# Early w_ada products on TensorE, late ones on VectorE, projections begun on the first half of the positions, and bias tables made for all heads at once

## What is computed

```
def first_block(x, c, w_ada, b_ada, ...):
    mod = (c @ w_ada[l] + b_ada[l])[:, None, :]            # 1024 -> 6 * 1024
    sh_m, sc_m, gt_m, sh_f, sc_f, gt_f = jnp.split(mod, 6, axis=-1)
    h = rms_norm(x, g_pre_mix[l]) * (1.0 + sc_m) + sh_m
    z = h @ w_in[l]
    u, f, q, k, v = jnp.split(z, splits, axis=-1)
    y = concatenate([s5_mixer(u), fourier_mixer(f), window_attention(q, k, v)]) @ w_out[l]
    x = x + gt_m * rms_norm(y, g_post_mix[l])
    h = rms_norm(x, g_pre_ffn[l]) * (1.0 + sc_f) + sh_f
    ...                                                     # gated FFN with a convolution
def second_block(x, p, rel_bias, ...):
    ...                                                     # swiglu
    z = rms_norm_2(h, attn_pre_g[i]) @ w_in[i] + b_in[i]
    out_a = sink_swa_gqa(...)                               # 8 heads, band of 128
    out_b = dilated_mixture(...)                            # 8 heads, three dilated bands
    ...                                                     # w_out, swiglu, gated embedding
```

## Time and profile before

| | us |
|---|---|
| median of 3 runs | 4137.23 |
| lowest, highest | 4129.18, 4148.82 |
| the profiled execution's own time | 4134.44 |
| its span, first to last instruction | 4132.2 |
| mean granted TensorE clock | 0.921 of full |

### The profile page before, as it was taken

The page is one execution under the profiler, slowest core; times in us unless marked ns, Lnnn a source line. Parts: engine busy times, 40 slices in busy tenths (PEclk is TensorE's granted clock), DMA queues, the critical chain, the costliest instruction groups (busy, mean ns, idle before and its releaser), DMA issues.

```text
span 4132.2 us, 41174 instructions
## 1 busy us (share of the span) xinstructions
PE 3422.3 (83%) x15967; PEld 2832.5 (69%) x15967; DVE 1255.2 (30%) x1716; ACT 800.0 (19%) x1416; POOL 1625.7 (39%) x830
## 2 busy tenths in 40 slices
PE   3755233787999989989999998987777899999977
PEld 2654233566888878868888786876666788878865
DVE  6603556335233332130000123115544200011233
ACT  3011000433111112020000122016541200000222
POOL 4777866014233336523322563210015123335633
PEclk9977666799999999999999999989999999999988
DMA  5333000333111123311111332343433111123332
GB/s 181 125 107 99 7 7 7 87 125 102 41 51 51 51 97 112 102 53 49 51 51 43 136 122 85 133 145 93 109 103 121 41 51 41 51 74 115 115 140 86
DMA packets 249780, 347.06 MB, mean 84 GB/s; under 512 B 12390, under 2 KB 190865, under 8 KB 249650
## 3 DMA queue, kind: packets, MB, share of 16 engines
q1 hardware_dynamic: 212530, 237.95, 19.3%
q10 hardware_dynamic: 31712, 89.34, 5.8%
q0 software_dynamic: 5408, 18.02, 1.5%
HBM read 289.30 MB, written 55.95 MB: 84 GB/s over the span
## 4 chain that ended last, share of the span: by engine, by line
PE 72%; DVE 12%; ACT 5%; POOL 5%; issue 4%; DMA 1%; SPq 0%; ACTq 0%; DVEq 0%; POOLq 0%
PE PS L727 65%; PE PS L1703 3%; DVE pt L630 1%; POOL lacc L344 1%; DVE ot L1459 1%; DVE px L633 1%; DVE h_lo L716 1%; DVE pl_ab L1809 1%; POOL lw L342 1%; PE PS L1411 1%; DMA ada<-w_ada 1%; DVE oo L1460 1%; ACT act L608 1%; POOL act L342 1%; ACT ph_ab L1748 1%
## 5 line engine op out<-in xcount | busy, mean ns | idle before, releaser
L225 POOL CAST w_hi<-w_raw 128x2048 fp32r<-128x2048 f32 x173 | 335.5, 1939 | 1762.7 <-DMA w_raw<-ffn_w_gu 668.1
L227 POOL TENSOR_TENSOR w_lo<-w_raw,w_hi 128x2048 fp32r<-128x2048 f32 x181 | 859.5, 4749 | 36.6 <-ACT w_hi L1176 11.7
L727 PE MATMUL PS<-h_hi,w_hi 128*128 128x512 f32 x2464 | 763.4, 391 | 16.3 <-DVE h_lo L721 10.0
L727 PE MATMUL PS<-h_lo,w_hi 128*128 128x512 f32 x2464 | 762.1, 391 | 0.0
L727 PE MATMUL PS<-h_hi,w_lo 128*128 128x512 f32 x2464 | 761.0, 390 | 0.0
L727 PEld LDWEIGHTS PS<-h_hi,w_hi 128*128 128x128 f32 x2464 | 463.8, 189 | 113.4 <-issue 10.2
L727 PEld LDWEIGHTS PS<-h_lo,w_hi 128*128 128x128 f32 x2464 | 464.9, 189 | 96.8
L727 PEld LDWEIGHTS PS<-h_hi,w_lo 128*128 128x128 f32 x2464 | 464.1, 188 | 96.7
L727 PE MATMUL PS<-w_hi,a_hi 128*128 128x512 f32 x1056 | 328.6, 393 | 25.2 <-DVE a_lo L793 25.2
L936 DVE TENSOR_TENSOR aT<-act,PS 128x1024 f32 (+1 forms) x44 | 53.7, 1221 | 911.1 <-ACT act L916 911.1
L727 PE MATMUL PS<-w_lo,a_hi 128*128 128x512 f32 x1056 | 328.1, 392 | 0.0
(11 more groups left out here) (292 smaller groups left out, 4476.5 us busy)
## 6 DMA issues: line engine op xcount, KB each, us to landing
w_raw<-ffn_w_gu SPq DMA_DIRECT2D x88, 512.0 KB, 4.9
w_raw<-ffn_w_down SPq DMA_DIRECT2D x88, 512.0 KB, 4.2
w_raw<-w_up SPq DMA_DIRECT2D x44, 512.0 KB, 4.7
w_raw<-w_down SPq DMA_DIRECT2D x44, 512.0 KB, 4.2
xs<-px ACTq DMA_DIRECT2D x40, 512.0 KB, 3.0
px<-xs ACTq DMA_DIRECT2D x5, 4096.0 KB, 14.4
w_raw<-w_out SPq DMA_DIRECT2D x32, 512.0 KB, 4.5
w_raw<-w_in SPq DMA_DIRECT2D x28, 512.0 KB, 5.5
```

Source lines behind the costliest of these rows:

```text
L225: e.tensor_copy(w_hi[b][:, 0:n], w_raw[b][:, 0:n]).then_inc(S("w_hi"), 1)
L227: e.tensor_tensor(w_lo[b][:, 0:n], w_raw[b][:, 0:n], w_hi[b][:, 0:n].bitcast(F32), ALU.subtract)\
L727: mm = e.matmul(o, a[ai], b[bi], start=start and first, stop=stop and end)
```

## The change

1. The early 16 tiles are multiplied on TensorE: the columns of c go into `cz`, [128, 8, 2, 2], with the other half zero, and 32 matmuls with two output rows, 512 columns each, add both parts up in two PSUM banks. VectorE copies the two rows, eight small transposes make columns of them. `ada_dve` and two `mod_pe` go.
2. The late tiles are VectorE's (`late_dve`): one operation a tile in place of two. Their loads go from GpSimd's queue to SP's, between the loads of chunks (`late_sp`).
3. The norms ahead of both projections use eight PSUM banks, and the first two slots of the projections are done for positions 0 to 511 first; the last four sets of transposes come behind the first of these.
4. The tables: one product for all 16 heads (heads as rows), four pieces; two stores with the source row repeated 128 times.
5. Second attention: head 0's (and head 1's q) loads are issued on SP during the projections; ScalarE waits for the last stores after its first exp. `vbias` moves.

```
-        def late_pool(e, v):
...
+        def late_sp(e, first, end):
+            for i in range(first, end):
+                if i < 2:
+                    e.wait_ge(S("ht_lo"), 16)
+                else:
+                    e.wait_ge(S("lacc"), i - 1)
+                v, k = 2 + i // 8, i % 8
+                e.dma_start(lw[i % 2][:], t["w_ada"][0][k * P:(k + 1) * P, v * D:(v + 1) * D]).then_inc(S(f"lw_ld{i % 2}"), 16)
+
+        def late_dve(e, v):
+            if v > 2:
+                e.wait_ge(S("mod_mm"), v - 2)
             for k in range(KT):
                 i = (v - 2) * 8 + k
                 e.wait_ge(S(f"lw_ld{i % 2}"), 16 * (i // 2 + 1))
...
-                    e.tensor_scalar(lw[i % 2][:], lw[i % 2][:], vcol("c", k), None, ALU.mult).then_inc(S("lw_c"), 1)
-                    e.wait_ge(S("lw_c"), (v - 2) * 7 + k)
-                    e.tensor_tensor(lacc[:], lacc[:], lw[i % 2][:], ALU.add).then_inc(S("lacc"), 1)
+                    e.wait_ge(S("lacc"), i)
+                    e.scalar_tensor_tensor(lacc[:], lw[i % 2][:], vcol("c", k), lacc[:], ALU.mult, ALU.add)\
+                     .then_inc(S("lacc"), 1)
...
-            for i in range(2):
-                e.wait_ge(S("ada_c"), 8 * i + 8)
-                mod_pe(e, acc[i], PS[:, 7 - i, 0:8])
+            e.wait_ge(S("cz"), 3)
+            for i in range(16):
+                if i % 4 == 0:
+                    e.wait_ge(S(f"ada_ld{i // 4}"), 64)
+                for h in range(2):
+                    mm = e.matmul(PS[0:2, 6 + h, :], cz[:, i % 8, 1 - i // 8, :], ada[i][:, h * 512:(h + 1) * 512],
+                                  start=i == 0, stop=i == 15)
+            mm.then_inc(S("ada_mm"), 1)
+            for q in range(4):
+                norm_set(e, 0, q)
+            e.wait_ge(S("md2"), 1)
+            for k in range(KT):
+                mm = e.transpose(PS[:, 4, k * 2:k * 2 + 2], mod2[:, k * P:(k + 1) * P], ident[0:2, 0:2])
+            mm.then_inc(S("md_t"), 1)
+            for q in range(4, 12):
+                norm_set(e, 0, q)
...
         def z_pe(e, z):
-            e.wait_ge(S("ht_lo"), 16 * (1 if z == 0 else 4))
+            n = 0 if z == 0 else 3
+            first = [s for s in slots[0:2]]
+            for h in range(2):
+                for w, (c, _, c0, width, _, _, _) in enumerate(first):
...
+                    e.wait_ge(S("ht_lo"), n * 16 + 8 + 8 * h)
+                    for k in range(KT):
+                        mm = three(e, [PS[:, 2 * w + h, :]], ...)
+                    if h == 0 and w == 0:
+                        for q in range(12, 16):
+                            norm_set(e, n, q)
...
-        PIECES = [(h, c, min(c + 512, w)) for h in range(16) for w in [W_A if h < 8 else W_B] for c in range(0, w, 512)]
+        PIECES = [(0, 0, W_A)] + [(1, c, min(c + 512, W_B)) for c in range(0, W_B, 512)]
...
+            for k, w in enumerate((W_A, W_B)):
+                r = slice(8 * k, 8 * k + 8)
+                e.dma_start(tabd[r, :, 0:w], tst[k][r, :].unsqueeze(1).to_broadcast([8, P, w])).then_inc(S("tb_st"), 16)
...
         def out_act(e, p):
-                e.wait_ge(S("tb_st0"), 128)
-                e.wait_ge(S("tb_st1"), 128)
+                e.wait_ge(S("tb_st"), 32)
...
+        def att_first_sp(e, s, a):
+            e.wait_ge(S("tb_st"), 32)
+            ...
+            att_load_k(e, s, a, 0)
+            att_load_q(e, s, a, 0)
+            att_load_q(e, s, a, 1)
+            ...
+            att_load_v(e, s, a, 0)
...
             @block.sync
-                stream_load(e, NBUF, G_OUT1[0] + 2)
+                late_sp(e, 0, 2)
+                stream_load(e, NBUF, G_DFT)
+                late_sp(e, 2, 10)
+                stream_load(e, G_DFT, G_DFT + 1)
+                late_sp(e, 10, 18)
+                stream_load(e, G_DFT + 1, G_DFT + 2)
+                late_sp(e, 18, 26)
+                stream_load(e, G_DFT + 2, G_DFT + 4)
+                late_sp(e, 26, 32)
+                stream_load(e, G_DFT + 4, G_OUT1[0] + 2)
...
             @block.gpsimd
-                stream_split(e, 0, NBUF)
-                late_pool(e, 2)
...
-                stream_split(e, 5, G_GLU)
+                stream_split(e, 0, G_GLU)
...
             @block.vector
                 chain_dve(e)
+                late_dve(e, 2)
                 z_dve(e, 0)
```

More of the change, by code:

```diff
@@ L384, in gates_pe @@
             e.transpose(PS[0:16, 5, 0:P], gain1[:, 16:32], ident[:]).then_inc(S("gr_t"), 1)
[L386 to L396, removed]
         def mod_dve(e, n, v, src):
@@ L415, in prep_dve @@
             e.tensor_copy(vec[:, 0:NV], PS[:, 6, 0:NV]).then_inc(S("vc"), 1)
+            e.memset(cz[:], 0.0).then_inc(S("cz"), 1)
+            e.wait_ge(S("cz"), 1)
             e.wait_ge(S("vc"), 1)
-            ada_dve(e, 0)
+            for v in range(2):
+                e.tensor_copy(cz[:, :, v, v], vec[:, VC["c"]:VC["c"] + KT]).then_inc(S("cz"), 1)
             norm0_rows_dve(e)
@@ L421, in prep_dve @@
             e.tensor_scalar(cc[1][:], PS[:, 5, 0:SSM_W], -1.0, None, ALU.mult).then_inc(S("cc"), 1)
[L422 to L425, removed]
+            e.wait_ge(S("ada_mm"), 1)
+            e.tensor_copy(mod2[:], PSr[0:2, 3072:4096]).then_inc(S("md2"), 1)
+            e.wait_ge(S("md_t"), 1)
+            e.tensor_tensor(mod[:, 0:16].rearrange("p (v k) -> p k v", v=2), PS[:, 4, 0:16].rearrange("p (k v) -> p k v", v=2),
+                            vec[:, VC["b_ada"]:VC["b_ada"] + 16].rearrange("p (v k) -> p k v", v=2), ALU.add)\
+             .then_inc(S("mod_v"), 1)
+            e.wait_ge(S("mod_v"), 1)
             gain_pre_dve(e, 0, 1, "g_pre_mix")
@@ L672, in norm0_rows_dve, with norm_bank, norm_set @@
                 norm_scale_dve(e, 0, T)
-        def norm_pe(e, n):
-            for hf in range(2):
+        def norm_bank(n, q):
+            return q % 4 + (4 * (q // 8) if n in (0, 3) else 0)
+        def norm_set(e, n, q):
+            hf, k = q // KT, q % KT
+            if k == 0:
                 e.wait_ge(S("m_xn"), n * 4 + (hf + 1) * 2)
@@ L679, in norm_pe @@
                     e.wait_ge(S("n_tmp"), n * 8 - 2 if hf == 0 else n * 8)
[L680 to L688, removed]
+            if k >= 4 or (hf and n not in (0, 3)):
+                e.wait_ge(S("ht_f"), n * 16 + q - 3)
+                if n > 1:
+                    e.wait_ge(S("ht_lo"), n * 16 + q - 3)
+            for i in range(4):
+                mm = e.transpose(PS[:, norm_bank(n, q), i * P:(i + 1) * P], xn[:, hf * 4 + i, k * P:(k + 1) * P], ident[:])
+            mm.then_inc(S("ht_t"), 1)
+        def norm_pe(e, n):
+            for q in range(12 if n == 3 else 16):
+                norm_set(e, n, q)
         def norm_out_act(e, n):
@@ L1652, in att_sp @@
                 return
-            for par in range(2):
-                e.wait_ge(S(f"tb_st{par}"), 128)
-            for h in range(len(s.heads)):
+            for h in range(2, len(s.heads)):
                 att_load_k(e, s, a, h)
@@ L1769, in att_act @@
             exps(0)
+            for par in range(2):
+                e.wait_ge(S(f"z_st{par}"), z_stores(s.z, par))
             for m in range(s.n):
```

85 lines of the change are left out of this document (42 added, 43 removed).

## The result

The changed kernel takes 4046.87 us (median of 4 executions, 4039.11 to 4053.31) against 4143.02 of the kernel before in the same comparison: the ratio is 0.9773 with a 95% interval of 0.9754 to 0.9792. That is 2.3% faster: 96 us between the medians, 90 us between the two profiled executions (spans of 4132.2 and 4041.9). The forecast was 150 us less, 3985, and its range ended at 4045.

A forecast was written before the change was run, and what follows sets the result against it. GpSimd was taken to bound the first 400 us, mostly TensorE at full rate after. Terms -111 - 24 + 2 - 4 - 13 = -150 us from 4134.4 gave 3985; range 3945 to 4045.

The forecast's parts named there:

- Part 5: First attention's bias tables: 32 pieces become 4, -24 us; two added stores stay hidden, +2 us for crowding.
- Rival E: The two table stores run at 51 GB/s, end at 911 us, x comes 10 us late: 3993 us, chance 0.15.
- Parts 1 to 4: Start to the last Fourier product: -111 us, bounds -125 and -85, ending at 288 instead of 399.1 us.
- Part 1: Early w_ada products, moved to TensorE: the gain is there at 68 us, 7 us earlier.
- rival A: Early w_ada products: TensorE stays at 1.2 GHz, gain at 92 instead of 68 us: 4010 us, chance 0.10.
- Part 2: First projections start after 8 instead of 16 transposed sets, at 77 instead of 93.2 us; slot 7 at 157.
- Part 3: Late w_ada products on VectorE, 2.9 us a tile: projections stage ends near 212 instead of 296 us, 84 us less.
- rival B: Late w_ada tiles keep GpSimd's pace, 5.8 us; last Fourier chunk ends at 382: 4079 us, chance 0.07.
- Part 4: Fourier stage: DFT products begin at 229 us, chunk 9's load is late in SP's queue, last product at 288.
- Part 6: Second block: half start before the second projections, -4 us; head 0 loaded early for the second attention, -13 us.
- Rival C: The two table stores go through one engine of sixteen, x comes 207 us late: 4190 us, chance 0.03.
- D: Bias tables: the pieces filled TensorE's gaps, or the clock falls, and nothing is gained: 4009 us, chance 0.10.

The follow-up runs named there:

- tab_spread: Changed kernel with each head's table row made on 16 partitions, so the stores read all 128 partitions; 4003.5 us, ratio 0.9669 to the kernel before.
- tab_ports: tab_spread with the table stores reading eight partitions again, 16 apart instead of neighbours; 4007.6 us in one execution.
- tab_old: Changed kernel with the bias tables made as before (32 pieces, 16 stores from 128 partitions each); 4037.0 us, ratio 0.9768 to the kernel before.
- ada_dve: Changed kernel with the early w_ada products on VectorE again; Fourier stage ended at 305.5 us against 305.0, whole 4058.0 us in one execution.
- no_half: Changed kernel with both projections waiting for all 16 transposed sets again; Fourier stage ended at 300.6 us, whole 4032.7 us in one execution.
- best4: Changed kernel with tab_spread, sp_order and act_order together, without the half start in the first projections; 3996.9 us, ratio 0.966 to the kernel before.
- late_pool: Changed kernel with the late w_ada tiles back on GpSimd between its splits; Fourier stage ended at 388.8 us, whole 4129.3 us in one execution.
- act_order: Changed kernel with ScalarE's first two w_hi of the Fourier stage moved behind the eight copies into bd; 4040.4 us, ratio 0.9762 to the kernel before.
- sp_order: Changed kernel with DFT chunk 9's load ahead of the last six late loads in SP's queue, these in pairs between chunks; 4026.1 us, ratio 0.9718 to before.
- no_first: Changed kernel with head 0's loads of the second attention issued behind the stores again; 4054.1 us in one execution.

## Why the prediction was wrong

It forecast -150 us and -90 came. The direction and the main mechanism were right, and two terms of the sum were not.

**Part 5, 37 us, the larger miss.** The step that failed is "Hidden; I take +2 for crowding". The stores' time was bounded, from 15 to 246 us, and one figure was read off a store from 16 partitions, "at worst a third of the rate, some 50 us". It was 123 us. The two rows behind the figure, 60 KB and 192 KB, both landed in 1.9 us, so they tell no rate. Rival E had this rate, 51 GB/s, and even so its price, 3993, was 54 us too low (17 of them are parts 1 to 4). What was wrong is the way of pricing: it asked only when the stores end and whether x waits for them. They ended at 818 us and x did not wait. What they cost came while they ran: the loads of `tab_bi`, on SP's queue, took 24 us for 5, and ScalarE stood 10 us in the issue. tab_spread and tab_ports tie this to the stores: same place, same bytes, other source partitions, and the loads land in 4.8 and 12.4 us, the stretch takes 43 and 36 us less. That the loads are late because they share DMA engines with the stores is an inference: no record here names an engine. The other half of part 5 was sized low: 28 pieces gave 31 to 36 us, not 24.

**Parts 1 to 4, 17 us.** They are told step by step:
- Part 1 was right in its own terms (gain 69.2 for 68, 64.4 in tab_old; rival A, the low clock throughout, did not come) and worth little by the end of the Fourier stage: ada_dve. Part 2's first half brought nothing that shows there: no_half and best4. The step that failed is "So TensorE hardly stops": the sum counted 16 us of an earlier start down to the Fourier stage. It took VectorE's chain as 46 us from 85 on; it was 53 from 91.7 on, because the half start itself delays VectorE's last splits and GpSimd splits two chunks beside the small operations, not one. That made TensorE wait 4.9 us at slot 7 (3.4 to 4.9 in the five executions of the same code) and run its next matmuls at the low clock (granted 0.50 from 163.4 to 167 us): the projections ended 7 us late, in tab_old and tab_spread 2.
- Part 3's pace was right (2.4 to 3.1 us a tile for 2.9), and rival B (5.8 us) fell: late_pool shows 84 us for it.
- Part 4: 22.0 us instead of 17 from the projections to the first DFT product. The two w_hi of ScalarE were priced at 2 us and cost 4.1 (act_order); 2 of the other 3 are an issue on ScalarE's queue ahead of them. Then 63.7 us instead of 59. The gap behind SP's queue was foreseen, at 10 us, and was 13.9; its undoing gives 8 us (sp_order).

**Part 6** was right: -3.0 and -10.0 for -4 and -13; no_half shows the first, as 3 us or more, and no_first the second. Rival C (one engine) did not come. D's outcome, that part 5 gains nothing, did come, but not for its reason: the pieces were dearer than forecast, and the stores took more than their removal gave.

**Left open.** Why the stretch between the Fourier stage and the first attention takes 374 to 380 us in some executions and 386 to 388 in others; its +2.3 us in the first table lie within that. What parts 1 and 2 bring together, now that VectorE has the late products, was not run.

## What to carry to other kernels

When a transfer is made cheaper to issue, ask from which partitions its bytes come, and price it by what else uses the DMA engines while it runs, not only by who waits for its end. A rate read off another store may hold only for the partitions and the size of that store. And where two engines wait for each other, an earlier start of the one is worth little until the other's whole work up to the meeting point, in any order, is shorter: count that before counting the start.

## What the runs showed of the hardware

- The same 6.29 MB in the same 2048 rows: 51 GB/s from 8 neighbouring partitions, 98 from 8 partitions 16 apart, and 331 (19 us) from 128.
- The issue of a store of 1024 rows held ScalarE for 8.97 us while an earlier store from 8 neighbours ran, for 4.87 us with both stores from partitions 16 apart, and for 1.22 us with both from all 128.
- While that store ran, loads of 192 KB on SP's queue landed in 24 us, against 12.4 with partitions 16 apart and 4.8 with 128.
- An operation of VectorE that falls beside GpSimd's `w_lo` (4.6 to 5.5 us) can take about as long as that: 5.41 us for 1.28, and 4.66 for 0.28.
- TensorE's granted clock in the first attention was 0.77 with two waits of 15 and 16 us and 0.96 without: the same matmuls took 80 and 72 us. In the 4 us behind the first wait it was 0.50, which is the 1.2 GHz level, and 1.00 from 755 us on.
